# Block two's up products: a shared normalised operand for the last 16 of 22 weight slabs

## The chip, the core and the metric

The kernel runs on one core of one Trainium2 chip. The metric is the device time in microseconds (us) of one execution; lower is better. The core has five engines that run side by side and meet at semaphores: TensorE (PE, matrix products), VectorE (DVE), ScalarE (ACT), GpSimd (Pool) and SyncE (SP, which issues the weight DMAs here).

## What is computed

Two transformer blocks of two layers each, batch 1, 256 tokens, width 1024, all in 32-bit floats. The change touches only block two, whose layer applies the same gated feed-forward (a "macaron" half) before and after its mixer; so there are four such half-layers in the program:

```python
def rmsnorm(x, g):
    return x * rsqrt(mean(x * x, -1) + NORM_EPS) * g
def swiglu_2(x, w_gate, w_up, w_down):
    return (silu(x @ w_gate) * (x @ w_up)) @ w_down
for l in range(2):
    f = swiglu_2(rmsnorm(h, ln_ffn1[l]) * (1 + sc1) + sh1, ffn1_wg[l], ffn1_wu[l], ffn1_wd[l])
    h = h + 0.5 * gt1 * f
    ...  # mixer
    f = swiglu_2(rmsnorm(h, ln_ffn2[l]) * (1 + sc3) + sh3, ffn2_wg[l], ffn2_wu[l], ffn2_wd[l])
    h = h + 0.5 * gt3 * f
```

The inner width is 2816, that is 22 blocks of 128.

## The kernel before

Activations lie feature-major: 8 tiles of 128 features by 256 tokens (`k.hid`). A product in full precision is three products of split operands, written by `passes`: high by high, low by high, high by low. So every weight is split into a high and a low part. The weights come in slabs, in one fixed order over the whole program. For a slab, SP loads the raw weights, `act_hi` (L424) has ACT round them to the high part, `dve_lo` (L434) has DVE subtract to get the low part, and PE multiplies. There are 5 raw/low buffers and 3 high buffers.

Of each half-layer, 22 slabs are up slabs (128 gate columns and 128 up columns of the weights; 2 x 8 x 3 = 48 matmuls) and 16 are down slabs (33 matmuls each). PE fills two PSUM banks with an up slab, one with the gate half and one with the up half. There are two such pairs, and `pe_turn` lets PE begin slab t only once DVE has reported slab t-2 evacuated (`k.ev`).

The up products run before the norm is known. Their operand `k.x` (norm_in) is hidden times the modulation's scale, without the factor 1/rms of each token, and has two more columns that hold the shift. The products therefore have 258 columns, the last two of which are the shift's product with the weights. `dve_macaron` mends this for each slab i, from the 1/rms row `rstd`: two copies take the shift column (L1871), gate x rstd (L1872), up x rstd (L1873), after which `k.ev` is raised; ACT takes Silu with the shift as its bias (L1843); DVE adds the shift to the up half and multiplies by the gate (L1876); ACT copies to the high part (L1845) and then runs `act_hi` for a later slab; DVE subtracts for the low part (L1880), and begins the next turn with `dve_lo`, which waits for that `act_hi`.

Pool has only the sum of squares here (`pool_squares`, L1739), which it does while the down products run. Block one's second feed-forward (`dve_ffn_up`, `act_ffn_up`) has a normalised operand from the start; its products have 256 columns, ACT takes Silu straight from PSUM (L1155), and DVE multiplies Silu by the up half (L1174) and subtracts (L1178).

No scheduler is at work: each engine executes its instructions in the order in which these functions write them.

## Time and profile before

| what | us |
|---|---|
| median of 3 runs | 3343.29 |
| lowest, highest | 3340.78, 3350.56 |
| the profiled execution's own time | 3334.63 |
| its span, first to last instruction | 3333.3 |

The profile is of one execution, which is 8.7 us shorter than the median. Its mean granted TensorE clock is 0.943 of full speed. An engine's busy time says how long it had work; whether it sets the pace of a stretch is read from who waits for whom.

### The profile page before, as it was taken

The page shows a single profiled execution, that of the slowest core. Times are in us where ns is not written, and L with a number is a line of the kernel's source. Part 1 is how long each engine was busy: PE and PEld are TensorE (multiplying, and loading weights), DVE is VectorE, ACT ScalarE, POOL GpSimd, SP SyncE. Part 2 cuts the span into 40 slices and gives each one's busy share as a digit, 9 for nine tenths or more (in the row PEclk, how much of TensorE's full clock was granted, in tenths as well). Part 3 has the DMA queues.
Part 4 walks back from the last instruction along what each step waited for, and adds up shares of the span by engine and source line. Part 5 has one row for each costly group of instructions (what it writes and reads, how often), then busy time and mean ns, then how long its engine had stood idle before and what let it go on. Part 6 is the DMA issues. An engine that isn't in the chain of part 4 may idle for free.

```text
span 3333.3 us, 55236 instructions
## 1 busy us (share of the span) xinstructions
PE 3109.6 (93%) x23574; PEld 2900.9 (87%) x23574; DVE 2133.2 (64%) x3166; ACT 1198.8 (36%) x1533; POOL 275.8 (8%) x283
## 2 busy tenths in 40 slices
PE   7899999799999799899999989999999998999999
PEld 4777878699999777899899989889999998897998
DVE  5676776776677677555665854466656575545664
ACT  2112122344444233444444411444444442134543
POOL 5000000110102021101001020000000101000101
PEclk9889999799999899899999989999999998999999
DMA  7253443488999656466556612336575562222654
GB/s 271 89 178 106 154 142 94 147 247 242 253 249 281 220 165 207 133 178 190 150 159 165 171 32 71 99 117 177 157 198 156 162 173 68 65 84 82 181 161 126
DMA packets 746225, 524.77 MB, mean 157 GB/s; under 512 B 19242, under 2 KB 711660, under 8 KB 745852
## 3 DMA queue, kind: packets, MB, share of 16 engines
q1 hardware_dynamic: 741852, 516.18, 53.9%
q0 software_dynamic: 4128, 5.06, 0.5%
q8 instruction: 186, 3.05, 0.4%
q14 instruction: 59, 0.48, 0.0%
HBM read 520.07 MB, written 2.94 MB: 157 GB/s over the span
## 4 chain that ended last, share of the span: by engine, by line
PE 46%; issue 18%; DVE 10%; ACT 8%; DMA 1%; POOL 1%; SPq 0%; DVEq 0%; ACTq 0%; POOLq 0%
PE bank L454 11%; PE bank L456 11%; PE bank L455 11%; ACT weights_hi L424 6%; PE bank L1296 2%; DVE weights_lo L434 1%; ACT mac_gate L1843 1%; DVE mac_prod L1876 1%; DVE side_sums L541 1%; PE bank L2211 1%; PE bank L2223 1%; PE bank L2219 1%; PE bank L562 1%; DVE mac_gate L1872 1%; PE bank L1316 1%
## 5 line engine op out<-in xcount | busy, mean ns | idle before, releaser
L434 DVE TENSOR_TENSOR weights_lo<-weights_raw,weights_hi 128x2048 fp32r<-128x2048 f32 (+3 forms) x414 | 852.8, 2061 | 388.6 <-ACT weights_hi L424 388.4
L424 ACT ACTIVATE weights_hi<-weights_raw 128x2048 fp32r<-128x2048 f32 (+3 forms) x414 | 709.1, 1714 | 737.2 <-PE bank L456 663.1
L454 PE MATMUL bank<-norm_in_hi,weights_hi 128*128 128x258 f32 x1408 | 406.6, 289 | 16.1 <-DVE mac_prod L1873 10.4
L456 PE MATMUL bank<-norm_in_hi,weights_lo 128*128 128x258 f32 x1408 | 399.1, 283 | 0.0
L455 PE MATMUL bank<-norm_in_lo,weights_hi 128*128 128x258 f32 x1408 | 398.5, 283 | 0.0
L454 PE MATMUL bank<-ffn_in_hi,weights_hi 128*128 128x256 f32 x1184 | 348.0, 294 | 19.5 <-DVE ffn_in_lo L1088 8.6
L455 PE MATMUL bank<-ffn_in_lo,weights_hi 128*128 128x256 f32 x1184 | 344.0, 291 | 0.0
L456 PE MATMUL bank<-ffn_in_hi,weights_lo 128*128 128x256 f32 x1184 | 343.9, 290 | 0.0
L454 PE MATMUL bank<-mix_in_hi,weights_hi 128*128 128x256 f32 x960 | 286.2, 298 | 15.5 <-DVE conv_in L2090 6.4
L454 PEld LDWEIGHTS bank<-norm_in_hi,weights_hi 128*128 128x128 f32 x1408 | 267.5, 190 | 28.4 <-issue 27.3
L455 PE MATMUL bank<-mix_in_lo,weights_hi 128*128 128x256 f32 x960 | 278.7, 290 | 0.0
L456 PE MATMUL bank<-mix_in_hi,weights_lo 128*128 128x256 f32 x960 | 278.1, 290 | 0.0
L455 PEld LDWEIGHTS bank<-norm_in_lo,weights_hi 128*128 128x128 f32 x1408 | 269.6, 191 | 0.0
L456 PEld LDWEIGHTS bank<-norm_in_hi,weights_lo 128*128 128x128 f32 x1408 | 267.4, 190 | 0.0
L454 PEld LDWEIGHTS bank<-ffn_in_hi,weights_hi 128*128 128x128 f32 x1184 | 234.5, 198 | 22.7 <-issue 18.5
L541 DVE SCALAR_TENSOR_TENSOR side_sums<-side_weights,silu_c,side_sums 128x512 f32<-128x512 f32 (+2 forms) x261 | 241.0, 981 | 4.9 <-DMA side_weights<-in_ada_w 4.4
L455 PEld LDWEIGHTS bank<-ffn_in_lo,weights_hi 128*128 128x128 f32 x1184 | 234.8, 198 | 0.1
L456 PEld LDWEIGHTS bank<-ffn_in_hi,weights_lo 128*128 128x128 f32 x1184 | 234.3, 198 | 0.0
L454 PEld LDWEIGHTS bank<-mix_in_hi,weights_hi 128*128 128x128 f32 x960 | 190.2, 198 | 19.5 <-issue 12.5
L454 PE MATMUL bank<-mac_hi,weights_hi 128*128 128x256 f32 x704 | 198.5, 282 | 0.8 <-DVE weights_lo L434 0.8
L456 PE MATMUL bank<-mac_hi,weights_lo 128*128 128x256 f32 x704 | 198.6, 282 | 0.0
L455 PE MATMUL bank<-mac_lo,weights_hi 128*128 128x256 f32 x704 | 198.5, 282 | 0.0
(422 smaller groups left out, 6932.8 us busy)
## 6 DMA issues: line engine op xcount, KB each, us to landing
weights_raw<-in_ffn_w SPq DMA_DIRECT2D x132, 512.0 KB, 5.5
weights_raw<-in_w_in SPq DMA_DIRECT2D x120, 512.0 KB, 5.1
side_weights<-in_ada_w SPq DMA_DIRECT2D x86, 576.0 KB, 4.2
weights_raw<-in_ffn_wg SPq DMA_DIRECT2D x88, 512.0 KB, 4.0
weights_raw<-in_ffn_wu SPq DMA_DIRECT2D x88, 512.0 KB, 5.3
weights_raw<-in_ffn_wd SPq DMA_DIRECT2D x64, 704.0 KB, 4.6
weights_raw<-in_ffn_w SPq DMA_DIRECT2D x48, 704.0 KB, 6.1
weights_raw<-in_ret_w_in SPq DMA_DIRECT2D x24, 1024.0 KB, 6.1
```

Of the source, the lines that this page charges most:

```text
L424: k.s.activation(k.w_hi[s % HIGHS][:, 0:n], k.raw[s % RING][:, 0:n], ACT.Copy).then_inc(*k.hi.up())
L434: k.v.tensor_tensor(k.w_lo[s % RING][:, 0:n], k.raw[s % RING][:, 0:n], k.w_hi[s % HIGHS][:, 0:n].bitcast(F32), ALU.subtract).then_inc(*k.l ...
L454: k.te.matmul(out, l[0], r[0], start=first, stop=False)
L455: k.te.matmul(out, l[0], r[1], start=False, stop=False)
L456: return k.te.matmul(out, l[1], r[0], start=False, stop=last)
L541: k.v.scalar_tensor_tensor(acc, buf, col, acc, ALU.mult, ALU.add).then_inc(*raised.up())
L562: m = k.te.matmul(bank[:, v * n + c:v * n + c + 1], sums[:, v * width + c * P:v * width + (c + 1) * P], k.ones[:, 0:1], start=True, stop=True)
L1296: k.te.matmul(bank[:, 0:n], k.pair_q[r, tt * P:(tt + 1) * P], k.pair_k[r, 0:n], start=True, stop=False)
L1316: m = k.te.matmul(bank[r, 0:T], k.pair_v_all[:, s, self.at(e, n)], k.pair_pt[:, e, s, :], start=s == 0, stop=s == 3)
L1843: s.activation(g, g, ACT.Silu, bias=k.shifted[:, c:c + 1]).then_inc(*k.gated.up())
L1872: v.tensor_tensor(g, bank[0][:, 0:T], rstd, ALU.mult).then_inc(*k.gate_scaled.up())
L1876: v.scalar_tensor_tensor(x, x, k.shifted[:, (i % 2) * 2 + 1:(i % 2) * 2 + 2], g, ALU.add, ALU.mult).then_inc(*k.prod_ready.up())
```

## The change

For slabs 0 to 5 (`LATE = 6`) the products are as before. Behind them the normalised and modulated operand is made once, into new tiles mac_in_hi and mac_in_lo (`k.xn`), and slabs 6 to 21 use it, with 256 columns. Pool makes hidden x rstd for each of the 8 feature tiles (into `k.sq`, squares). ACT makes scale x that + shift twice, once rounded (mac_in_hi) and once in full (mac_in, `k.xv`, four buffers), two feature tiles at the end of each of its turns 0 to 3. The low part is a subtraction: of even tiles on Pool, of odd tiles on DVE at the end of its turns 1 to 4. For slabs 6 to 21 DVE and ACT then do what block one's second feed-forward does. The buffers that hold the operand are new; nothing else moves.

```diff
@@ -39,6 +39,7 @@
 NLEV = 7
 FILLS = 11
 BA_AT = 4
+LATE = 6
 LN_AT = {1: 8, 2: 3}
 TRI = 3 * P
 
@@ -341,6 +342,8 @@
         self.ln_added = self.sig("ln_added", "pool")
         self.ln_inverted = self.sig("ln_inverted", "dve")
         self.ln_spread = self.sig("ln_spread", "pe")
+        self.times_rms = self.sig("times_rms", "pool")
+        self.xn_lo = self.sig("xn_lo", "pool")
         self.slabs = weight_slabs(a)
         self.at_slot, self.side_at, self.side_prev = [], [], [None, None]
         self.sides = side_plan(a)
@@ -1820,7 +1823,11 @@
             pe_norm(k)
             continue
         for c in range(2):
-            m = feature_major(k, bank[c][:, 0:T + 2], w, c * P, x, slice(0, T + 2))
+            if i < LATE:
+                m = feature_major(k, bank[c][:, 0:T + 2], w, c * P, x, slice(0, T + 2))
+            else:
+                m = feature_major(k, bank[c][:, 0:T], w, c * P, k.xn, slice(0, T),
+                                  ready=(lambda n: (k.norm_lo if n % 2 else k.xn_lo).at(n // 2 + 1)) if i == LATE and c == 0 else None)
             if i == 1 and c == 0:
                 pe_spread(k)
         m.then_inc(*k.used.up())
@@ -1834,16 +1841,31 @@
         m.then_inc(*k.used.up())
 
 
-def act_macaron(k, following):
+def act_macaron(k, layer, j, following):
     s = k.s
+    sh = 3 * j * KD
     act_std(k)
     for i in range(KF):
         g, c = k.gate[i % 2][:, :], (i % 2) * 2
-        s.wait_ge(*k.gate_scaled.at(i + 1))
-        s.activation(g, g, ACT.Silu, bias=k.shifted[:, c:c + 1]).then_inc(*k.gated.up())
-        s.wait_ge(*k.prod_ready.at(i + 1))
+        if i < LATE:
+            s.wait_ge(*k.gate_scaled.at(i + 1))
+            s.activation(g, g, ACT.Silu, bias=k.shifted[:, c:c + 1]).then_inc(*k.gated.up())
+            s.wait_ge(*k.prod_ready.at(i + 1))
+        else:
+            s.wait_ge(*k.used.at(i + 1))
+            if i < LATE + 2:
+                s.wait_ge(*k.prod_ready.at(i - 1))
+            else:
+                s.wait_ge(k.ev.h, k.t0 + i - 1)
+            s.activation(g, k.GB[(k.t0 + i) % 2][0][:, 0:T], ACT.Silu).then_inc(*k.gated.up())
+            s.wait_ge(k.ev.h, k.t0 + i + 1)
         s.activation(k.mid[0][:, i, :], k.prod[i % 2][:, :], ACT.Copy).then_inc(*k.mid_hi.up())
         act_hi(k)
+        for n in (2 * i, 2 * i + 1) if 2 * i < KD else ():
+            sc, bi = (k.mods2[:, layer, at + n:at + n + 1] for at in (sh + KD, sh))
+            s.wait_ge(*k.times_rms.at(n + 1))
+            s.activation(k.xn[0][:, n, :], k.sq[:, n, :], ACT.Identity, scale=sc, bias=bi)
+            s.activation(k.xv[:, n % 4, :], k.sq[:, n, :], ACT.Identity, scale=sc, bias=bi).then_inc(*k.norm_hi.up())
     for i in range(4 * KD // 2):
         act_hi(k)
         if i % 4 == 1:
@@ -1861,12 +1883,19 @@
         dve_lo(k)
         if i == 0:
             dve_rms(k)
-            v.tensor_copy(rstd, k.AB[1][:, 0:T]).then_inc(*k.dve.up())
-            v.wait_ge(*k.dve.now())
+            v.tensor_copy(rstd, k.AB[1][:, 0:T]).then_inc(*k.affine.up())
+            v.wait_ge(*k.affine.at(1))
         turn = k.t0 + i
         bank, g, x = k.GB[turn % 2], k.gate[i % 2][:, :], k.prod[i % 2][:, :]
         v.wait_ge(*k.used.at(i + 1))
         v.wait_ge(*k.mid_lo.at(i - 1))
+        if i >= LATE:
+            v.wait_ge(*k.gated.at(i + 1))
+            v.tensor_tensor(x, g, bank[1][:, 0:T], ALU.mult).then_inc(*k.ev.up())
+            v.wait_ge(k.ev.h, turn + 1)
+            v.wait_ge(*k.mid_hi.at(i + 1))
+            v.tensor_tensor(k.mid[1][:, i, :], x, k.mid[0][:, i, :].bitcast(F32), ALU.subtract).then_inc(*k.mid_lo.up())
+            continue
         for c in range(2):
             v.tensor_copy(k.shifted[:, (i % 2) * 2 + c:(i % 2) * 2 + c + 1], bank[c][:, T:T + 1])
         v.tensor_tensor(g, bank[0][:, 0:T], rstd, ALU.mult).then_inc(*k.gate_scaled.up())
@@ -1878,6 +1907,11 @@
         v.wait_ge(*k.prod_ready.at(i + 1))
         v.wait_ge(*k.mid_hi.at(i + 1))
         v.tensor_tensor(k.mid[1][:, i, :], x, k.mid[0][:, i, :].bitcast(F32), ALU.subtract).then_inc(*k.mid_lo.up())
+        if 1 <= i <= KD // 2:
+            n = 2 * i - 1
+            v.wait_ge(*k.norm_hi.at(n + 1))
+            v.tensor_tensor(k.xn[1][:, n, :], k.xv[:, n % 4, :], k.xn[0][:, n, :].bitcast(F32), ALU.subtract).then_inc(
+                *k.norm_lo.up())
     for i in range(4 * KD // 2):
         dve_lo(k)
         if i % 2 == 1:
@@ -1893,6 +1927,16 @@
 
 
 def pool_macaron(k):
+    g, rstd = k.g, k.stat[0][:, 0:T]
+    g.wait_ge(*k.affine.at(1))
+    for n in range(KD + 2):
+        if n < KD:
+            g.tensor_tensor(out=k.sq[:, n, :], in0=k.hid[:, n, :], in1=rstd, op=ALU.mult).then_inc(*k.times_rms.up())
+        if n >= 2 and n % 2 == 0:
+            i = n - 2
+            g.wait_ge(*k.norm_hi.at(i + 1))
+            g.tensor_tensor(out=k.xn[1][:, i, :], in0=k.xv[:, i % 4, :], in1=k.xn[0][:, i, :].bitcast(F32),
+                            op=ALU.subtract).then_inc(*k.xn_lo.up())
     pool_squares(k, 1)
 
 
@@ -2635,9 +2679,11 @@
     m.at = inner
     k.mid = [m.take("mac_hi" + tag, [P, KF, T], F32R), m.take("mac_lo" + tag, [P, KF, T], F32R)]
     k.gate = [m.take(f"mac_gate{i}_{tag}", [P, T]) for i in range(2)]
+    k.xn = [m.take("mac_in_hi" + tag, [P, KD, T], F32R), m.take("mac_in_lo" + tag, [P, KD, T], F32R)]
+    k.xv = m.take("mac_in" + tag, [P, 4, T])
     k.prod = [m.take(f"mac_prod{i}_{tag}", [P, T]) for i in range(2)]
     sp_macaron(k)
-    act_macaron(k, following)
+    act_macaron(k, layer, j, following)
     dve_macaron(k, layer, j, following)
     pool_macaron(k)
     pe_macaron(k)
```


On DVE, a turn of a late slab before (names: weights_lo is `dve_lo`, ret_decay the shift columns, mac_gate, mac_prod and mac_lo the gate, the product and its low part; in brackets the semaphores it waits for):

```order
L434 TENSOR_TENSOR weights_lo_55<-weights_raw_50,weights_hi_59 128x2048 [waits weights_hi_ready]
L1871 COPY ret_decay<-bank 128x1 [waits mid_lo,weights_used]
L1871 COPY ret_decay<-bank 128x1
L1872 TENSOR_TENSOR mac_gate_00_15585<-bank,stat_69 128x256
L1873 TENSOR_TENSOR mac_prod_00_15587<-bank,stat_69 128x256
L1876 SCALAR_TENSOR_TENSOR mac_prod_00_15587<-mac_prod_00_15587,ret_decay,mac_gate_00_15585 128x256 [waits gated,banks_evacuated]
L1880 TENSOR_TENSOR mac_lo_15584<-mac_prod_00_15587,mac_hi_15583 128x256 [waits mid_hi,prod_ready]
```

and a late turn now:

```order
L437 TENSOR_TENSOR weights_lo_55<-weights_raw_50,weights_hi_59 128x2048 [waits weights_hi_ready]
L1894 TENSOR_TENSOR mac_prod_00_15590<-mac_gate_00_15585,bank 128x256 [waits gated,mid_lo,weights_used]
L1897 TENSOR_TENSOR mac_lo_15584<-mac_prod_00_15590,mac_hi_15583 128x256 [waits mid_hi,banks_evacuated]
L437 TENSOR_TENSOR weights_lo_56<-weights_raw_51,weights_hi_60 128x2048 [waits weights_hi_ready]
L1894 TENSOR_TENSOR mac_prod_00_15591<-mac_gate_00_15586,bank 128x256 [waits gated,mid_lo,weights_used]
L1897 TENSOR_TENSOR mac_lo_15584<-mac_prod_00_15591,mac_hi_15583 128x256 [waits mid_hi,banks_evacuated]
L437 TENSOR_TENSOR weights_lo_57<-weights_raw_52,weights_hi_61 128x2048 [waits weights_hi_ready]
```

Six instructions between two weights_lo became two. mac_prod now waits for Silu (gated) ahead of it, and `k.ev` is raised by it.

On ACT, the end of turn 0 and turn 1 of a half-layer before:

```order
L1843 ACTIVATE mac_gate_00_15586<-mac_gate_00_15586,ret_decay 128x256 [waits gate_scaled]
L1845 ACTIVATE mac_hi_15583<-mac_prod_00_15588 128x256 [waits prod_ready]
L424 ACTIVATE weights_hi_61<-weights_raw_51 128x2048 [waits weights_used,weights_arrived2]
L1843 ACTIVATE mac_gate_00_15585<-mac_gate_00_15585,ret_decay 128x256 [waits gate_scaled]
L1845 ACTIVATE mac_hi_15583<-mac_prod_00_15587 128x256 [waits prod_ready]
```

and the end of turn 1 with turn 2 now:

```order
L1862 ACTIVATE mac_hi_15583<-mac_prod_00_15591 128x256 [waits prod_ready]
L427 ACTIVATE weights_hi_61<-weights_raw_51 128x2048 [waits weights_used,weights_arrived2]
L1867 ACTIVATE mac_in_hi_15587<-squares,modulation_68 128x256 [waits times_rms]
L1868 ACTIVATE mac_in_15589<-squares,modulation_68 128x256
L1867 ACTIVATE mac_in_hi_15587<-squares,modulation_68 128x256 [waits times_rms]
L1868 ACTIVATE mac_in_15589<-squares,modulation_68 128x256
L1852 ACTIVATE mac_gate_00_15585<-mac_gate_00_15585,ret_decay 128x256 [waits gate_scaled]
L1862 ACTIVATE mac_hi_15583<-mac_prod_00_15590 128x256 [waits prod_ready]
L427 ACTIVATE weights_hi_59<-weights_raw_52 128x2048 [waits weights_used,weights_arrived3]
```

Four instructions now stand between weights_hi and the next turn's mac_gate.

On Pool, all that a half-layer adds, ahead of the sum of squares:

```order
L1934 TENSOR_TENSOR squares<-hidden_both,stat_69 128x256 [waits affine]
L1934 TENSOR_TENSOR squares<-hidden_both,stat_69 128x256 x2
L1938 TENSOR_TENSOR mac_in_lo_15588<-mac_in_15589,mac_in_hi_15587 128x256 [waits norm_hi]
L1934 TENSOR_TENSOR squares<-hidden_both,stat_69 128x256 x2
L1938 TENSOR_TENSOR mac_in_lo_15588<-mac_in_15589,mac_in_hi_15587 128x256 [waits norm_hi]
L1934 TENSOR_TENSOR squares<-hidden_both,stat_69 128x256 x2
L1938 TENSOR_TENSOR mac_in_lo_15588<-mac_in_15589,mac_in_hi_15587 128x256 [waits norm_hi]
L1934 TENSOR_TENSOR squares<-hidden_both,stat_69 128x256
L1938 TENSOR_TENSOR mac_in_lo_15588<-mac_in_15589,mac_in_hi_15587 128x256 [waits norm_hi]
```

Three products go first; from then on each subtraction waits for ACT's tile (norm_hi), with two products behind it. Before, none of these rows was there.

## Rows read from the trace of the kernel before

**Rows 1.** Tile norm_in_hi: two lines' instructions (ns); last, an idle time (us, times) and what ended it.

```profile
L454 PE MATMUL bank<-norm_in_hi,weights_hi x1408: 276/284/583, 1589.1 to 3256.2; 128*128 128x258 f32 x176
...
L1712 ACT ACTIVATE norm_in_hi<-hidden_both,modulation x32: 490/494/509, 1585.8 to 3124.9; 128x256 fp32r<-128x256 f32 x32
...
  DVE mac_prod L1873: 10.4, 64
```

**Rows 2.** Windows, slabs 6 to 21 of the four half-layers: stretch, length, busy time by engine.

```profile
core 0: us, PE busy (x) PEld busy (x) DVE busy (x) ACT busy (x) POOL busy (x), PEclk, DMA share, GB/s
1628.39:1726.91 98.52, 96.08 (x768) 93.42 (x769) 63.80 (x113) 43.44 (x50) 0.00 (x0) 1.00 0.58 158
...
sum 394.15, PE 384.39 PEld 373.78 DVE 255.16 ACT 173.83 POOL 0.00; mean PE 96.10 PEld 93.45 DVE 63.79 ACT 43.46 POOL 0.00
```

**Rows 3.** Windows: slabs 2 and 3 of the first half-layer; slabs 6-21 of block one.

```profile
1604.88:1616.42 11.54, 11.54 (x98) 11.54 (x97) 7.73 (x14) 4.95 (x5) 0.00 (x0) 1.00 0.67 183
1413.89:1505.03 91.14, 91.14 (x771) 91.14 (x769) 49.57 (x48) 41.18 (x48) 0.00 (x0) 1.00 0.63 174
```

**Rows 4.** Timeline of DVE, one turn: start, length, engine, line, instruction, idle before.

```profile
1606.63 2.29 DVE L434 TENSOR_TENSOR weights_lo<-weights_raw,weights_hi 128x2048 fp32r<-128x2048 f32 x1 [1.31 <-ACT weights_hi L424]
1608.84 0.21 DVE L1871 COPY ret_decay<-bank 128x1 f32<-128x1 f32 x2
1608.97 0.41 DVE L1872 TENSOR_TENSOR mac_gate<-bank,stat 128x256 f32<-128x256 f32 x1
1609.30 0.41 DVE L1873 TENSOR_TENSOR mac_prod<-bank,stat 128x256 f32<-128x256 f32 x1
1610.03 0.49 DVE L1876 SCALAR_TENSOR_TENSOR mac_prod<-mac_prod,ret_decay,mac_gate 128x256 f32<-128x256 f32 x1 [0.32 <-ACT mac_gate L1843]
1611.07 0.43 DVE L1880 TENSOR_TENSOR mac_lo<-mac_prod,mac_hi 128x256 fp32r<-128x256 f32 x1 [0.55 <-ACT mac_hi L1845]
1612.80 2.29 DVE L434 TENSOR_TENSOR weights_lo<-weights_raw,weights_hi 128x2048 fp32r<-128x2048 f32 x1 [1.31 <-ACT weights_hi L424]
```

**Rows 5.** Timeline of ACT, the same turn.

```profile
1609.42 0.51 ACT L1843 ACTIVATE mac_gate<-mac_gate,ret_decay 128x256 f32<-128x256 f32 x1 [2.83 <-DVE mac_gate L1872]
1610.55 0.42 ACT L1845 ACTIVATE mac_hi<-mac_prod 128x256 fp32r<-128x256 f32 x1 [0.62 <-DVE mac_prod L1876]
1610.87 1.90 ACT L424 ACTIVATE weights_hi<-weights_raw 128x2048 fp32r<-128x2048 f32 x1
```

**Rows 6.** Timeline of DVE in block one's second feed-forward.

```profile
1454.38 0.42 DVE L1174 TENSOR_TENSOR ffn_prod<-ffn_gate,bank 128x256 f32<-128x256 f32 x1 [0.69 <-ACT ffn_gate L1155]
...
1457.09 2.29 DVE L434 TENSOR_TENSOR weights_lo<-weights_raw,weights_hi 128x2048 fp32r<-128x2048 f32 x1 [1.30 <-ACT weights_hi L424]
```

**Rows 7.** Timeline of ACT there, the same turn.

```profile
1453.97 0.38 ACT L1155 ACTIVATE ffn_gate<-bank 128x256 f32<-128x256 f32 x1 [2.60 <-PE bank L456]
1454.84 0.42 ACT L1157 ACTIVATE ffn_hi<-ffn_prod 128x256 fp32r<-128x256 f32 x1 [0.49 <-DVE ffn_prod L1174]
1455.16 1.90 ACT L424 ACTIVATE weights_hi<-weights_raw 128x2048 fp32r<-128x2048 f32 x1
```

**Rows 8.** Timeline, down products of the first half-layer: one Pool addition beside VectorE.

```profile
1736.90 1.62 DVE L434 TENSOR_TENSOR weights_lo<-weights_raw,weights_hi 128x1408 fp32r<-128x1408 f32 x1
...
1737.57 1.54 POOL L1739 TENSOR_TENSOR square_sum<-square_sum,stat 128x256 f32<-128x256 f32 x1 [138.39 <-ACT stat L1714]
```

**Rows 9.** Lines 1725, 1739 and 434: duration min/median/max in ns.

```profile
L1725 DVE SCALAR_TENSOR_TENSOR norm_in_lo<-hidden_both,modulation,norm_in_hi x32: 473/479/964, 1588.5 to 3125.4; 128x256 fp32r<-128x256 f32 x32
...
L1739 POOL TENSOR_TENSOR square_sum<-square_sum,stat x56: 721/1467/2539, 1586.7 to 3320.9; 128x256 f32<-128x256 f32 x56
...
L434 DVE TENSOR_TENSOR weights_lo<-weights_raw,weights_hi x414: 285/2286/2831, 50.6 to 3309.6; 128x2048 fp32r<-128x2048 f32 x92, 128x1408 fp32r<-128x1408 f32 x37, 128x1024 fp32r<-128x1024 f32 x6, 128x1536 fp32r<-128x1536 f32 x3
```

**Rows 10.** Windows: 16 down slabs of the first half-layer, then of block one.

```profile
1726.91:1790.10 63.19, 62.98 (x530) 62.66 (x528) 33.70 (x31) 27.62 (x27) 13.42 (x7) 1.00 0.71 199
1510.73:1573.40 62.67, 62.67 (x531) 62.67 (x530) 33.31 (x30) 25.69 (x24) 10.17 (x10) 1.00 0.71 201
```

## Prediction

> **What bounds the kernel now.** I first asked which stretch the change can reach. It edits the up slabs 6 to 21 of four half-layers, and the windows give them: 98.52 us in the first, 394.15 in all four, 98.54 on the mean, at full granted clock [rows 2]. That is 12% of the span. TensorE executes there all the time by its busy column, so next I asked whether anything makes it wait. The tile view says yes: before 64 of the matmuls, the first of slabs 6 to 21 four times over, it sat until DVE's mac_prod (L1873), the instruction that frees a bank pair [rows 1]. The idle time shown, 10.4 us, understates it, because the modelled end of the matmul ahead covers part of each wait. A slab without the wait tells more: slabs 2 and 3 take 11.54 / 2 = 5.77 us [rows 3], while one turn from weights_lo to weights_lo takes 1612.80 - 1606.63 = 6.17 us [rows 4]. So PE loses 0.40 us a slab. It starts with a lead that the first five slabs use up; from slab 6 on it runs at the pace of the others.
>
> Which others? The timelines of DVE and ACT read together show one closed ring [rows 4, 5]: weights_lo to the shift copies 2.21, to mac_gate 0.13, to Silu's start on ACT 0.45, to the DVE multiply 0.61, to ACT's mac_hi 0.52, to weights_hi 0.32, to the next weights_lo 1.93. The sum is 6.17. Neither engine is full (DVE 63.80 of 98.52 us, ACT 43.44 [rows 2]); they wait for each other in turn.
>
> **What a late turn costs now.** Block one's second feed-forward executes the same instructions in the same order as the new late turns, with the same 48 matmuls of 256 columns. There Silu to DVE's product is 0.41, to ffn_hi 0.46, to weights_hi 0.32, to weights_lo 1.93 and through it 2.21 to 2.29 [rows 6, 7]. Two readings follow. The ring itself is 2.21 + 0.46 + 0.32 + 1.93 = 4.92 us, if Silu is done in time. From a slab's last matmul, the whole tail up to the end of weights_lo is 5.33 to 5.41 us. Both lie under what PE needs, so PE sets the pace, and the trace agrees: 16 slabs in 91.14 us, 5.70 each, with PE busy for all of it [rows 3]. The DMA is no obstacle to that pace: it moved 174 GB/s there, 158 in the stretch to be changed.
>
> Of the 0.47 to 0.48 us gained per slab, 0.40 is the wait and 0.075 the two columns (5.77 against 5.696, which is 1.6 ns a matmul). The Trainium skill ("TensorE: Matmul & The Clock Gate", Back-to-back issue gap) prices a column at 1/2.4 ns, so two would give 0.83 ns a matmul, and the columns of the whole change some 2 us less than I count; the measured slabs decide, and the sum goes by them.
>
> **Which slabs gain.** Slab 6 may start only when slab 4 is evacuated, and slab 7 only after slab 5, and both evacuations are old turns. Slab 6 thus still takes 6.17. The first new evacuation, that of slab 6, comes some 5.7 us after slab 7 began (from the end of mac_prod to the next weights_lo 3.09, then 2.21 and a product of 0.42 [rows 4, 6]), just when slab 8 can begin. So slabs 7 to 21 run at PE's pace: before, 98.54 - 6.17 = 92.37 us; after, 15 x 5.696 = 85.44. Gain 6.9 us per half-layer.
>
> **The start of the down products.** Because DVE is a slab behind, the old kernel's second and third down slabs wait for it. 16 down slabs took 63.19 us against 62.67 in block one, where DVE is not behind [rows 10]. Gain 0.5.
>
> **What is added, and where it lies.** ACT: four more activations in each of turns 0 to 3. The nearest row, the same kind on one tile with a scale, is 0.49 us [rows 1], so 2.0 us, behind weights_hi and ahead of the next Silu, where ACT sits idle for 2.83 [rows 5]: free, with 0.8 to spare, provided that Pool's products are there. DVE: one subtraction of 0.43 in turns 1 to 4, in the 1.31 that it idles before weights_lo [rows 4]: free. Its last one (tile 7) ends 1611.07 - 1609.30 + 2 x 0.43 - 0.41 = 2.2 us after slab 6 starts, and slab 6 asks for tile 7 after 21 of its matmuls, 2.5 us in (5.70 / 48 each): just in time, and if late, it is hidden by the 0.40 that slab 7 waits anyway.
>
> Pool: 8 products and 4 subtractions, 0.72 us each when undisturbed [rows 9]. Pool has nothing else there. Its price is what it does to DVE. Pool's addition at 1737.57 took 1.54 and ended 0.59 after the weights_lo beside it (1738.52) [rows 8]: it was held until that ended. The other way round, the DVE instruction with two SBUF inputs at L1725 takes 0.479 and up to 0.964 [rows 9], held by a Pool instruction in progress. In turns 1 to 3 Pool's subtraction is released while weights_lo executes, so it and two products (one in turn 3) start as weights_lo ends, a burst of some 2.2 us; the DVE multiply of the ring (L1876) starts 1.2 us after weights_lo ends, inside the burst. In turn 0 it meets the first three products. So four turns of five lose between 0 and 0.49 us; I take 0.40, as a burst back to back leaves hardly a gap: 1.6 us a half-layer. Such a loss delays the evacuation of slab 5, which slab 7 waits for, so it counts in full. The bounds: nothing if Pool always yields, and 4 x (0.49 + 0.55) = 4.2 if weights_lo is held as well each time (its maximum is 2831 ns over a median of 2286 [rows 9]).
>
> **Sum.** (6.9 + 0.5 - 1.6) x 4 = 23.2 us. The profiled execution of 3334.6 would become 3311.4; it lies 8.7 below the median of the three runs, and I apply the same saving to the median: 3343.3 - 23.2 = 3320.1. The bounds give 3343.3 - 29.6 = 3313.7 and 3343.3 - 12.8 = 3330.5.
>
> **Rivals.**
> - *Pool in DVE's way at full price.* Each early turn loses in both places: 4.2 a half-layer, 3330.5. For it speaks that weights_lo has been caught at 2831 ns; against it that Pool waits for ACT's tile when weights_lo begins, and is idle. The Trainium skill ("GPSIMD Engine Reference", Key points) says that Pool shares its SBUF interfaces with VectorE and contends with instructions that have two SBUF inputs, which would name both L1876 and weights_lo; the trace agrees that such instructions are held.
> - *Slower: the operand comes late.* ACT executes in order. If Pool's products reach it after weights_hi, its four activations hold the next Silu, and the ring grows by the lateness, in each of turns 1 to 3, and slab 6 waits as well. In turn 1 ACT asks for product 3 when weights_hi ends, 1612.77 [rows 5]; the burst starts at 1608.92 [rows 4] and product 3 is second in it, so it leaves at 1610.4, 2.4 us early. Each Pool instruction would have to take over 1.9 us instead of 0.72 for lateness to start, and the loss passes the gain of 7.4 a half-layer only when three turns and slab 6 lose 1.85 us each. The median of Pool's additions is 1.467 [rows 9], but beside long DVE instructions such as that of [rows 8], which the burst doesn't meet. With 3 us lost at each of the four places: 3343.3 + 4 x (12 - 7.4) = 3362.
> - *No change.* Another wait takes the place of the old one at the late slabs (a low part, a DMA) and holds the pace at about 6.1: 3340. Block one's 16 slabs without any wait speak against it.
> - *Pool always yields.* 3313.7.
>
> **How the numbers follow.** My forecast, the new pace with a small Pool loss (3314 to 3327), has 0.78; Pool at full price 0.12; no change 0.05; slower 0.05. For the range I take both bounds of the Pool cost, 3313.7 and 3330.5, and widen them by about 2 us, since the medians of three runs scatter (3340.78 to 3350.56): 3311 to 3333. That leaves out no change and slower. A measurement of this kernel tells 0.3% (10 us) from nothing; a saving of 12.8 still passes it. Faster 0.89, same 0.07, slower 0.04.
>
> **What the new profile would show.** Late slabs at 5.70 us, about 91.6 us for 16 of them in place of 98.5; the waits for mac_prod down from 64 to about 8 (slabs 6 and 7 of each half-layer); Silu's activation waiting for PE and not for DVE; L1876's early ones up to 0.96 us where Pool is active; Pool some 35 to 70 us busier, DVE busy less. The prediction is wrong if slabs 7 to 21 still wait, if ACT's Silu in turns 1 to 4 starts late behind the four activations, or if slab 6 waits for mac_in_lo by more than 0.4 us.

## The result, and the profile after

The changed kernel took 3307.34 us (median of 4 executions, 3298.29 to 3315.22), the kernel before 3346.93 beside it (4 executions, 3340.78 to 3350.98): a ratio of 0.9882, with a 95% interval of 0.9851 to 0.9914. It is 1.2% faster. That is the forecast direction, but more than the range allowed: 3307.3 lies 3.7 us below its lower end of 3311. The profiled execution took 3305.93, its span is 3304.6; before, it took 3334.63, so the two are 28.7 apart. Three executions of the kernels below took 4777 (both_orders), 7402 (late14) and 7754 us (both_again), for no known reason; they count in the medians of the table but not in its ratios, and the last is the one that both_again's profile fell on.

The page's head shows the engines' busy time and the shares of the chain that ended last:

```profile
span 3304.6 us, 55108 instructions
...
PE 3090.1 (94%) x23574; PEld 2892.9 (88%) x23574; DVE 2082.5 (63%) x2926; ACT 1220.6 (37%) x1597; POOL 330.6 (10%) x331
...
PE 55%; issue 14%; DVE 9%; ACT 4%; DMA 2%; POOL 1%; SPq 0%; DVEq 0%; ACTq 0%; POOLq 0%
```

Pool is 54.8 us busier than the 275.8 of before (48 instructions more), DVE 50.7 less than its 2133.2, PE 19.5 less than its 3109.6. Pool and DVE stand in the prediction's list of what the profile would show. So do early multiplies of DVE (L1876, now L1905) of up to 0.96 us, and these didn't come: the longest took 0.58. In the chain PE rose to 55% from 46%.

The windows of slabs 6 to 21 answer to [rows 2]. Shown are the first half-layer and the sum of all four:

```profile
core 0: us, PE busy (x) PEld busy (x) DVE busy (x) ACT busy (x) POOL busy (x), PEclk, DMA share, GB/s
1634.53:1726.29 91.76, 91.54 (x769) 91.35 (x770) 52.77 (x56) 42.65 (x51) 0.00 (x0) 1.00 0.61 170
...
sum 367.02, PE 366.00 PEld 365.28 DVE 211.01 ACT 170.55 POOL 0.00; mean PE 91.50 PEld 91.32 DVE 52.75 ACT 42.64 POOL 0.00
```

16 slabs take 91.75 us where they took 98.54; the prediction said about 91.6. DVE's busy time fell from 63.80 to 52.77. The down products of the first half-layer answer to [rows 10]:

```profile
1726.29:1789.10 62.81, 62.81 (x530) 62.60 (x528) 31.15 (x25) 25.99 (x25) 13.69 (x7) 1.00 0.72 202
```

They take 62.81 instead of 63.19: 0.4 gained, where the prediction said 0.5. The tile view of the new operand answers to [rows 1]:

```profile
L457 PE MATMUL bank<-mac_in_hi,weights_hi x1024: 274/281/360, 1634.5 to 3228.1; 128*128 128x256 f32 x171
...
  DVE mac_prod L1902: 1.0, 4
...
  ACT mac_gate L1860: 110.0, 48
```

The waits for DVE's product fell from 64 to 4 (the prediction said about 8). Those four are the starts of slab 7. At slab 6 the view shows no wait, since the modelled end of the matmul ahead covers it; but slab 6 starts 0.40 after that matmul, where matmuls otherwise start 0.12 apart. Silu (L1860) now waits for PE, 48 times of 64, and no longer for DVE. So the engines have changed roles, as expected: PE sets the pace, and ACT and DVE wait for it. PE's own timeline, cut into slabs, gives from slab 4 on of the first half-layer 5.88, 6.13, 6.22, 5.76, 5.72, and then 5.70 each (before: 5.79 for slab 4, and about 6.18 from slab 5 on). A slab's length includes the wait ahead of the next, so that 6.22 holds slab 7's.

How DVE comes from the old pace to the new one shows in its timeline in the middle of the stretch:

```profile
1668.27 2.29 DVE L437 TENSOR_TENSOR weights_lo<-weights_raw,weights_hi 128x2048 fp32r<-128x2048 f32 x1 [1.31 <-ACT weights_hi L427]
1670.48 0.41 DVE L1894 TENSOR_TENSOR mac_prod<-mac_gate,bank 128x256 f32<-128x256 f32 x1
...
1673.18 2.29 DVE L437 TENSOR_TENSOR weights_lo<-weights_raw,weights_hi 128x2048 fp32r<-128x2048 f32 x1 [1.31 <-ACT weights_hi L427]
1675.73 0.42 DVE L1894 TENSOR_TENSOR mac_prod<-mac_gate,bank 128x256 f32<-128x256 f32 x1 [0.26 <-ACT mac_gate L1860]
```

From weights_lo to weights_lo it takes 1673.18 - 1668.27 = 4.91 us, the new ring of 4.92. It still catches up there, 0.79 a slab. One turn later the product waits for Silu, and Silu for PE: from about slab 12 on DVE is no longer behind.

**Where all of the gain is.** The four half-layers, each from its first up matmul to the end of its down products, took 201.11, 197.77, 198.38 and 197.74 us before, 795.0 together, and take 193.92, 190.57, 190.54 and 190.57 now, 765.6. That is 29.4 us less. 0.65 of it isn't the change's: the third one's down products were slower before (3.96 us a slab in place of 3.92). The medians differ by 39.6, so the question is what the rest of the program did. Windows of the three stretches outside, of before:

```profile
0.00:1589.08 1589.08, 1452.79 (x9511) 1303.63 (x9511) 1081.01 (x1386) 521.57 (x670) 163.70 (x190) 0.93 0.63 186
1790.19:2254.90 464.71, 430.52 (x3836) 408.73 (x3837) 280.45 (x506) 162.03 (x235) 26.28 (x25) 0.94 0.36 101
2650.89:3122.10 471.21, 436.18 (x3836) 414.13 (x3837) 280.27 (x506) 161.97 (x235) 26.39 (x25) 0.92 0.36 100
sum 2525.00, PE 2319.49 PEld 2126.49 DVE 1641.73 ACT 845.58 POOL 216.37; mean PE 773.16 PEld 708.83 DVE 547.24 ACT 281.86 POOL 72.12
```

And of after:

```profile
0.00:1595.18 1595.18, 1458.46 (x9511) 1309.66 (x9511) 1080.88 (x1386) 521.77 (x670) 162.96 (x190) 0.92 0.63 186
1789.10:2251.92 462.82, 428.40 (x3837) 407.19 (x3838) 280.47 (x506) 161.94 (x235) 26.28 (x25) 0.94 0.37 102
2632.86:3100.68 467.82, 433.02 (x3837) 411.12 (x3837) 280.04 (x506) 162.05 (x235) 26.36 (x25) 0.93 0.36 101
sum 2525.82, PE 2319.88 PEld 2127.97 DVE 1641.38 ACT 845.76 POOL 215.60; mean PE 773.29 PEld 709.32 DVE 547.13 ACT 281.92 POOL 71.87
```

Single stretches move by 6 us up and 3 down, the sum by 0.8. Outside the half-layers nothing was gained. The ten us between 29.4 and 39.6 are what these few executions happened to take; the two profiled ones differ by 28.7.

### The profile page after: what moved, and what is told of

Same layout as the page of the kernel before. It is cut to its first block, busy times and chain, and to the rows that moved or that the text cites. A ratio compares the mean times of both kernels' runs of the same rounds, so it can differ in the third digit from the quotient of the medians.

```text
span 3304.6 us, 55108 instructions
## 1 busy us (share of the span) xinstructions
PE 3090.1 (94%) x23574; PEld 2892.9 (88%) x23574; DVE 2082.5 (63%) x2926; ACT 1220.6 (37%) x1597; POOL 330.6 (10%) x331
## 4 chain that ended last, share of the span: by engine, by line
PE 55%; issue 14%; DVE 9%; ACT 4%; DMA 2%; POOL 1%; SPq 0%; DVEq 0%; ACTq 0%; POOLq 0%
PE bank L457 14%; PE bank L458 14%; PE bank L459 14%; ACT weights_hi L427 3%; PE bank L1299 2%; DVE weights_lo L437 1%; DVE side_sums L544 1%; PE bank L2255 1%; PE bank L2267 1%; PE bank L2263 1%; PE bank L565 1%; DVE side_sums_odd L544 1%; PE bank L1304 1%; DMA weights_raw<-in_ffn_w 1%; PE bank L1302 1%
## 5 line engine op out<-in xcount | busy, mean ns | idle before, releaser
L457 PE MATMUL bank<-mac_in_hi,weights_hi 128*128 128x256 f32 x1024 | 289.0, 282 | 1.5 <-DVE mac_prod L1902 1.0
L459 PE MATMUL bank<-mac_in_hi,weights_lo 128*128 128x256 f32 x1024 | 288.4, 282 | 0.0
L458 PE MATMUL bank<-mac_in_lo,weights_hi 128*128 128x256 f32 x1024 | 288.4, 282 | 0.0
L457 PEld LDWEIGHTS bank<-ffn_in_hi,weights_hi 128*128 128x128 f32 x1184 | 234.5, 198 | 23.2 <-issue 19.0
L457 PEld LDWEIGHTS bank<-mac_in_hi,weights_hi 128*128 128x128 f32 x1024 | 192.8, 188 | 2.9 <-issue 2.9
L459 PEld LDWEIGHTS bank<-mac_in_hi,weights_lo 128*128 128x128 f32 x1024 | 192.8, 188 | 0.0
L458 PEld LDWEIGHTS bank<-mac_in_lo,weights_hi 128*128 128x128 f32 x1024 | 192.8, 188 | 0.0
```

Source lines behind the costliest of these rows:

```text
L457: k.te.matmul(out, l[0], r[0], start=first, stop=False)
L458: k.te.matmul(out, l[0], r[1], start=False, stop=False)
L459: return k.te.matmul(out, l[1], r[0], start=False, stop=last)
```

## The experiments

Each ran beside the kernel before on the same chip. The stated half-layer is from the profile, and is one that the slower pace of PE (also at the end) doesn't touch; before it is 197.74 us long, after the change 190.56.

| kernel | median us (executions) | ratio to before, 95% | half-layer us |
|---|---|---|---|
| after_again | 3310.79 (6) | 0.9911, 0.9889 to 0.9933 | 190.54 |
| before_again | 3336.04 (12) | 0.9989, 0.9974 to 1.0005 | 197.73 |
| added_alone | 3340.47 (12) | 0.9995, 0.9984 to 1.0005 | 197.80 |
| order_alone | 3310.54 (5) | 0.9900, 0.9883 to 0.9917 | 190.71 |
| order_again | 3310.70 (5) | 0.9900, 0.9879 to 0.9922 | 190.71 |
| both_orders | 3309.36 (6) | 0.9898, 0.9874 to 0.9921 | 189.46 |
| both_again | 3310.85 (6) | 0.9886, 0.9861 to 0.9911 | none |
| late14 | 3336.05 (10) | 0.9980, 0.9962 to 0.9998 | 194.42 |
| late_wide | 3318.38 (5) | 0.9940, 0.9919 to 0.9962 | 191.71 |
| pool_shifted | 3317.29 (4) | 0.9929, 0.9905 to 0.9953 | 191.28 |
| pool_twice | 3310.57 (1) | one execution | 190.56 |
| pool_mid | 3313.12 (1) | one execution | 191.81 |

### How large is the gain: the two kernels once more

after_again is the changed kernel, before_again the one before, unchanged.

> The changed kernel once more, with more rounds. Theory 1: all of the gain lies in the four half-layers, which are 7.2, 7.2, 7.8 and 7.2 us shorter in the two profiles, 29.4 together; the ratio should come out near 1 - 29.4/3345 = 0.9912, and the rest of the 39.6 us between the medians is scatter. Theory 2: stretches outside the half-layers, the mixers above all, gain too: then about 38 to 40 us, ratio 0.9882, again.

> The kernel of before against itself: how far two medians of one kernel differ. Ratio 1.000; if the interval is wider than 0.003, the 10 us between the two theories of the size can't be told from it. The profile should repeat the four half-layers within 0.3 us, and differ by several us in the stretches between them, where the granted clock falls.

The half-layers came back as 193.93, 190.54, 190.55, 190.56 and as 201.11, 197.76, 197.73, 197.73: they repeat within 0.05 us. The one exception is the third of before, 198.38 and now 197.73: its down slabs ran at the slower pace the first time. The ratio 0.9911 stands for 29.7 us of 3342.4, the 29.4 of the half-layers. Another 10 us from elsewhere (0.9882) lie just outside its interval, and the windows above, where the rest of the program gained nothing, speak against them more strongly. The kernel before against itself gave 0.9989, with an interval of 0.0031: by the limit that its expectation sets, such a timing can hardly tell 10 us.

### The operand made, but not used

```diff
-LATE = 6
+LATE = 22
```

> LATE = 22: the operand is made (Pool, ACT, DVE) but no slab uses it, so every turn is an old one. Theory A (Pool costs next to nothing here): DVE's product at L1905 is held in turn 0 by 0.09 us and not in turns 1 to 3; a half-layer is longer by 0.1 us, the kernel by 0.4 us: ratio 1.000. Rival (as predicted, 0.40 in each of four turns): 6.4 us slower, ratio 1.002. What it says on the whole: the added work alone gives nothing.

Nothing is gained, and nothing is lost: slabs 6 to 21 take 98.52, and a half-layer 0.06 more than before. The view of the line that Pool can hold, L1905 (before: L1876), in this kernel:

```profile
L1905 DVE SCALAR_TENSOR_TENSOR mac_prod<-mac_prod,ret_decay,mac_gate x88: 483/485/578, 1606.5 to 3259.8; 128x256 f32<-128x256 f32 x88
```

Of 88 instructions the longest takes 0.578, 0.09 over the median, and it occurs in turn 0 of a half-layer alone. So the 12 instructions on Pool, 16 on ACT and 4 on DVE cost next to nothing, not the 1.6 us that I had put on Pool.

### The order of the instructions alone, without a new operand

The kernel before, with ACT's mac_hi behind the next weights_hi, and DVE's mac_lo behind the next weights_lo. So the DVE multiply and mac_hi no longer stand between Silu and weights_hi:

```diff
         s.activation(g, g, ACT.Silu, bias=k.shifted[:, c:c + 1]).then_inc(*k.gated.up())
+        act_hi(k)
         s.wait_ge(*k.prod_ready.at(i + 1))
         s.activation(k.mid[0][:, i, :], k.prod[i % 2][:, :], ACT.Copy).then_inc(*k.mid_hi.up())
-        act_hi(k)
...
-        dve_lo(k)
         if i == 0:
+            dve_lo(k)
             dve_rms(k)
...
+        if i < KF - 1:
+            dve_lo(k)
```

> The kernel of before with one reordering and no new operand: ACT rounds the next weights right behind Silu, ahead of mac_hi, and DVE makes their low part right behind L1876, ahead of mac_lo. If the ring of waits between DVE and ACT is the cause, it shrinks to Silu to weights_hi 0.45, to weights_lo 1.93, 2.21 through it, mac_lo 0.35, copies 0.13 and 0.13, to Silu 0.45: 5.65 us, below the 5.77 of a slab with 258 columns. Then PE sets the pace in all 22 slabs: 0.40 x 16 + 0.35 + 0.46 for the down products = 7.2 us a half-layer, 29 us, ratio 0.9914, without any of the change. Rival: what helps is that DVE and ACT have less to do or that the products are narrower; then a late slab stays at 6.18 and the time the same.

The window of slabs 6 to 21, and DVE's timeline while it still catches up:

```profile
1641.20:1733.58 92.38, 92.38 (x771) 92.38 (x770) 64.11 (x114) 40.83 (x48) 0.00 (x0) 1.00 0.61 169
```

```profile
1651.65 2.29 DVE L434 TENSOR_TENSOR weights_lo<-weights_raw,weights_hi 128x2048 fp32r<-128x2048 f32 x1 [1.25 <-ACT weights_hi L424]
...
1657.12 2.29 DVE L434 TENSOR_TENSOR weights_lo<-weights_raw,weights_hi 128x2048 fp32r<-128x2048 f32 x1 [1.25 <-ACT weights_hi L424]
```

And ACT's:

```profile
1654.78 0.51 ACT L1843 ACTIVATE mac_gate<-mac_gate,ret_decay 128x256 f32<-128x256 f32 x1 [2.85 <-DVE mac_gate L1872]
1655.19 1.90 ACT L424 ACTIVATE weights_hi<-weights_raw 128x2048 fp32r<-128x2048 f32 x1
```

The new ring is read off the starts: weights_lo and mac_lo up to the copies 1654.20 - 1651.65 = 2.55 (the copies start at 1654.20), copies and mac_gate to Silu 0.58, Silu 0.41, weights_hi 1657.12 - 1655.19 = 1.93. The sum is 5.47, and below PE's 5.77, at which all slabs from 2 on are. (I expected 5.65; 0.13 of that was a second step for the copies, which lies inside the other steps.) The half-layer gains 7.03 of the change's 7.18, and DVE does as much work as before (64.11 busy against 63.80 in [rows 2]). So what cost the 0.40 a slab was the length of the closed ring, which the order sets, and not how much DVE has to do. The new operand isn't needed for that.

### Both: the change with the early turns in that order

```diff
+            act_hi(k)
             s.wait_ge(*k.prod_ready.at(i + 1))
...
-        act_hi(k)
+        if i >= LATE:
+            act_hi(k)
...
-        dve_lo(k)
+        if i == 0 or i > LATE:
+            dve_lo(k)
...
+        dve_lo(k)
+        v.wait_ge(*k.prod_ready.at(i + 1))
+        v.wait_ge(*k.mid_hi.at(i + 1))
+        v.tensor_tensor(k.mid[1][:, i, :], x, k.mid[0][:, i, :].bitcast(F32), ALU.subtract).then_inc(*k.mid_lo.up())
```

> The changed kernel, with its six early turns reordered: weights_hi right behind Silu, weights_lo ahead of mac_lo, the extra subtraction ahead of weights_lo. Theory: slabs 4, 5 and 6 took 5.88, 6.13 and 6.22 us in the changed kernel because DVE is late there; now 5.77, 5.77 and 5.70: 1.0 us a half-layer, 4 us in all against the changed kernel, ratio to before about 0.990. Rival: the extra work in turns 1 to 4 (ACT 2.3 us, DVE 0.4, Pool in DVE's way) lengthens the reordered ring beyond 5.77; then slabs 4 to 6 stay near 6.1 and nothing is gained.

In the profile no slab from 2 on is held up: slabs 2 to 5 take 5.77, 6 to 21 take 5.70, and a half-layer 189.46, 1.1 less than the change and 1.25 less than the order alone. Slabs 6 to 21, with PE busy throughout:

```profile
1622.42:1713.55 91.13, 91.13 (x770) 91.13 (x769) 52.73 (x56) 42.41 (x50) 0.00 (x0) 1.00 0.62 171
```

Over four that is 761.2 against 766.2, 5 us. The executions can't tell it: the intervals of the two ratios overlap almost wholly. Both were run again with their own expectations:

> The new operand with reordered early turns once more, on the same chip as the reordering alone. By the half-layers of the profiles (192.8, 189.5, 189.5 and 189.5 us) it is 33 us faster than before, ratio 0.9901, and 5 us faster than the reordering alone: 1.3 us a half-layer from the narrower products.

> The reordering alone once more: by its half-layers (194.1, 190.7, 190.7 and 190.7 us) 28 us faster than before, ratio 0.9916. If the two can't be told apart in time, the intervals overlap and only the profiles separate them.

0.9886 and 0.9900, with intervals of 0.004 to 0.005 across: still not told apart. By the profile both_orders is the best kernel of the study; by the timing that stays open.

### Where in the stretch the gain comes from: only the last 8 slabs

```diff
-LATE = 6
+LATE = 14
```

> LATE = 14: eight of the sixteen late slabs are old ones again. Theory (gain per slab): slabs 6 to 13 go back to 6.18 and slab 14 is held as slab 6 is now, so 8 x 0.48 = 3.85 us a half-layer come back, 15.4 in all; the half-layers are 13.9 us shorter than before in place of 29.4. Rival (the gain lies in the end of the up products or outside them): the gain stays near the full one.

Windows of slabs 6 to 13 and 14 to 21 of the second half-layer:

```profile
2305.91:2355.30 49.39, 48.15 (x385) 46.73 (x385) 32.33 (x57) 21.82 (x25) 0.00 (x0) 1.00 0.63 171
2355.30:2401.50 46.20, 45.91 (x385) 45.73 (x385) 27.31 (x31) 21.78 (x27) 0.00 (x0) 1.00 0.56 155
```

The old slabs keep 6.17, the new ones take 5.77 on the mean, with their own slow first one (PE busy 45.91 of 46.20). This half-layer gained 3.35 of 7.20: the 3.85 of the eight slabs that stayed old came back as expected. The other three ran at PE's slower pace from the late slabs on (198.94, 195.56 and 195.51 us), so the profile has 10.6 us gained in all, not the 13.9 expected. The timing (0.9980, 6.7 us, with 12.7 us as the most that its interval allows) falls short of the 13.9 too. That is in part the slower pace; how much of it every execution had, the one profile doesn't show.

### What the two columns are worth

258 columns in the late slabs; the two extra are copied from the old operand, and their results are read by nobody.

```diff
-                m = feature_major(k, bank[c][:, 0:T], w, c * P, k.xn, slice(0, T),
+                m = feature_major(k, bank[c][:, 0:T + 2], w, c * P, k.xn, slice(0, T + 2),
...
+        if i == 0:
+            s.activation(k.xn[0][:, :, T:T + 2], k.x[0][:, :, T:T + 2].bitcast(F32), ACT.Copy)
...
+        if i == 1:
+            v.tensor_copy(k.xn[1][:, :, T:T + 2], k.x[1][:, :, T:T + 2].bitcast(F32))
```

> The changed kernel with 258 columns in the late slabs too (two idle columns, their content copied and never read); DVE and ACT have their new turns. Theory: a late slab takes 5.77 in place of 5.70, without waits: 16 x 0.075 = 1.2 us a half-layer, 4.8 in all. By the price of 1/2.4 ns a column it would be 16 x 48 x 0.83 ns = 0.64 a half-layer, 2.6 in all. If the columns were the main thing, the time would go back by over 20 us.

The window of its slabs 6 to 21 in the second half-layer:

```profile
2293.36:2386.27 92.91, 92.70 (x768) 92.53 (x769) 52.76 (x56) 42.70 (x51) 0.00 (x0) 1.00 0.61 168
```

92.91 against 91.75: 1.16 us for 768 matmuls, 1.5 ns each. Over the four half-layers the columns are 4.6 us of the 29.4, and the wait is the rest. The Trainium skill ("TensorE: Matmul & The Clock Gate", Back-to-back issue gap) gives 1/2.4 ns a column for an isolated matmul at full clock; an estimate from it is 0.83 ns for two columns, or 0.64 us for these 768 matmuls. The trace, where a weight load goes with each matmul, shows nearly twice that.

### Pool's price, by moving its burst

In the change Pool's subtraction is held by weights_lo, and its products follow. The timelines of Pool and of DVE in turns 0 and 1 of the first half-layer:

```profile
1608.78 2.34 POOL L1934 TENSOR_TENSOR squares<-hidden_both,stat 128x256 f32<-128x256 f32 x3 [5.64 <-DVE stat L1886]
1613.83 1.86 POOL L1938 TENSOR_TENSOR mac_in_lo<-mac_in,mac_in_hi 128x256 fp32r<-128x256 f32 x1 [2.71 <-ACT mac_in L1868]
1615.66 1.64 POOL L1934 TENSOR_TENSOR squares<-hidden_both,stat 128x256 f32<-128x256 f32 x2
```

```profile
1609.94 0.58 DVE L1905 SCALAR_TENSOR_TENSOR mac_prod<-mac_prod,ret_decay,mac_gate 128x256 f32<-128x256 f32 x1 [0.32 <-ACT mac_gate L1852]
...
1612.81 2.29 DVE L437 TENSOR_TENSOR weights_lo<-weights_raw,weights_hi 128x2048 fp32r<-128x2048 f32 x1 [1.31 <-ACT weights_hi L427]
...
1616.21 0.48 DVE L1905 SCALAR_TENSOR_TENSOR mac_prod<-mac_prod,ret_decay,mac_gate 128x256 f32<-128x256 f32 x1 [0.32 <-ACT mac_gate L1852]
...
1617.60 0.42 DVE L1913 TENSOR_TENSOR mac_in_lo<-mac_in,mac_in_hi 128x256 fp32r<-128x256 f32 x1
```

The subtraction takes 1.86, since it sits until weights_lo ends. The first product then starts at 1615.66, and L1905 at 1616.21, 0.55 later: it takes its plain 0.48. In turn 0 it starts 0.45 after the second of the three products, and takes 0.58. So what may count is the phase, by which I mean how long after the start of Pool's instruction DVE's starts. To test it, a memset on Pool (0.31 us) behind each subtraction delays the two products. (The edit, and those of the next two kernels, are against the changed kernel.)

```diff
+            g.wait_ge(*k.pool.now())
+            g.memset(k.square_sum[:, :], 0.0).then_inc(*k.pool.up())
+    g.wait_ge(*k.pool.now())
```

> The changed kernel with one Pool memset (0.31 us) behind each of Pool's subtractions, so that the two products that follow start later. Theory A: a Pool instruction holds DVE's instruction with two SBUF inputs only during its first 0.55 us; L1905 starts 0.55 after a Pool product in turns 1 to 3 by the accident of its place, 0.22 after it now, and should be held by 0.32 (0.80 us in place of 0.48) in those three turns: slab 7 starts 1.0 us later, 3.9 us in all. Theory B: Pool does not hold this instruction at all: L1905 stays at 0.48 in turns 1 to 3, and the time the same.

Pool's and DVE's timelines of pool_shifted in turn 2, and the line's minimum, median and maximum:

```profile
1620.74 0.31 POOL L1941 MEMSET square_sum<- 128x256 f32 x1
1621.01 1.64 POOL L1934 TENSOR_TENSOR squares<-hidden_both,stat 128x256 f32<-128x256 f32 x2
```

```profile
1621.31 0.73 DVE L1905 SCALAR_TENSOR_TENSOR mac_prod<-mac_prod,ret_decay,mac_gate 128x256 f32<-128x256 f32 x1 [0.31 <-ACT mac_gate L1852]
```

```profile
L1905 DVE SCALAR_TENSOR_TENSOR mac_prod<-mac_prod,ret_decay,mac_gate x24: 484/646/730, 1608.6 to 3150.1; 128x256 f32<-128x256 f32 x24
```

Now L1905 starts 1621.31 - 1621.01 = 0.30 after the product, and takes 0.73: held for 0.24. The half-layer is 0.72 longer, which is three turns of 0.24. I expected 0.22 and a hold of 0.32; the memset moved the products by 0.25 and not by 0.31, and 0.30 + 0.24 is 0.54, as 0.22 + 0.32 would have been.

With two memsets (`for _ in range(2)` ahead of the same two lines):

> Two memsets behind each of Pool's subtractions. One memset moved the two products by 0.25 us and L1905 was held by 0.24. Theory A (held until 0.54 us after the start of the Pool instruction, and only if it starts inside that time): the products start another 0.27 later, L1905 some 0.03 us after one of them, and is held by about 0.5 us (0.98 in place of 0.48) in turns 1 to 3: 1.5 us a half-layer, with turn 0 1.6, which is the 0.40 a turn that the prediction charged. If the product starts just after L1905, Pool waits instead and L1905 stays at 0.48. Theory B (the hold is a fixed 0.24 whenever they overlap): 0.72 again.

Line L1905 of pool_twice, and the timelines of DVE and Pool in turn 2:

```profile
L1905 DVE SCALAR_TENSOR_TENSOR mac_prod<-mac_prod,ret_decay,mac_gate x24: 483/486/574, 1604.4 to 3147.7; 128x256 f32<-128x256 f32 x24
```

```profile
1623.06 0.49 DVE L1905 SCALAR_TENSOR_TENSOR mac_prod<-mac_prod,ret_decay,mac_gate 128x256 f32<-128x256 f32 x1 [0.32 <-ACT mac_gate L1852]
```

```profile
1622.49 0.67 POOL L1942 MEMSET square_sum<- 128x256 f32 x2
1623.12 1.02 POOL L1934 TENSOR_TENSOR squares<-hidden_both,stat 128x256 f32<-128x256 f32 x1
```

L1905 is at its plain 0.486, and Pool waits: its product starts at 1623.12, just behind L1905 (1623.06), and takes 1.02 instead of 0.74. The half-layer is 190.56, the change's own. So in these runs whichever of the two started first went first.

With one memset of 256 columns and one of 32, the phase falls in between:

> Behind each of Pool's subtractions a memset of 256 columns and one of 32, so that the two products start later than with one full memset and earlier than with two. L1905 should then start 0.05 to 0.2 us after a Pool product starts. Theory A (held until 0.54 us after the start of the Pool instruction): L1905 takes 0.8 to 0.97 us in turns 1 to 3, a half-layer is 1.1 to 1.5 us longer than in the changed kernel. If the product still starts after L1905, it stays at 0.48.

```profile
L1905 DVE SCALAR_TENSOR_TENSOR mac_prod<-mac_prod,ret_decay,mac_gate x24: 485/736/914, 1610.9 to 3148.7; 128x256 f32<-128x256 f32 x24
```

```profile
1623.69 1.64 POOL L1934 TENSOR_TENSOR squares<-hidden_both,stat 128x256 f32<-128x256 f32 x2
```

```profile
1623.81 0.91 DVE L1905 SCALAR_TENSOR_TENSOR mac_prod<-mac_prod,ret_decay,mac_gate 128x256 f32<-128x256 f32 x1 [0.32 <-ACT mac_gate L1852]
```

By the records' starts the product begins 0.12 ahead of L1905, which takes 0.89 to 0.91 in turns 1 to 3, held for about 0.42; slabs 4 and 5 of the undisturbed half-layer take 6.60 and 6.55, and it is 1.25 longer than the change's. So a price near my 1.6 does exist, but at another phase than the change has.

## Why the prediction was right on the mechanism and wrong on the number

- **The bound**: right, though PE is busy for 96.08 of the 98.52 us by its busy column, and not all the time as I wrote. The ring of DVE and ACT held PE by 0.40 a slab. order_alone, which shortens that ring and nothing else, brings 5.77 us slabs.
- **The new ring of 4.92, and PE's pace of 5.70**: right; 4.91 was seen, and 91.75 for 16 slabs against some 91.6.
- **Which slabs gain**: right. Slab 6 takes 6.22 with slab 7's wait in it, and from slab 8 on PE is free. late14 gave back 3.85 us for eight slabs in its one half-layer at PE's full pace, as expected.
- **Start of the down products**: right, 0.4 to 0.5 where I said 0.5.
- **The two columns**: 1.5 ns a matmul against the 1.6 I counted.
- **ACT's four activations**: they start 0.49 apart, 2.0 us in all, though each takes 0.58 in the record, and 0.86 of idle time stays ahead of Silu where I said 0.8:

```profile
1612.68 0.58 ACT L1867 ACTIVATE mac_in_hi<-squares,modulation 128x256 fp32r<-128x256 f32 x1
1613.17 0.59 ACT L1868 ACTIVATE mac_in<-squares,modulation 128x256 f32<-128x256 f32 x1
...
1614.15 0.59 ACT L1868 ACTIVATE mac_in<-squares,modulation 128x256 f32<-128x256 f32 x1
1615.60 0.51 ACT L1852 ACTIVATE mac_gate<-mac_gate,ret_decay 128x256 f32<-128x256 f32 x1 [0.86 <-DVE mac_gate L1901]
```

- **Pool's price in DVE's way, 1.6 us a half-layer**: this is the step that failed, a term of the sum that was mis-sized. I wrote "I take 0.40, as a burst back to back leaves hardly a gap". It measured 0.1, in turn 0 alone. I had asked only whether the two overlap. What decides is when DVE's instruction starts inside Pool's: the hold fell from about 0.42 us at 0.12 us after Pool's start to 0.24 at 0.30, 0.09 at 0.45 and nothing at 0.55. The products start 0.56 after weights_lo ends, and L1905 1.11 after it, so they meet at 0.55 in each of turns 1 to 3. The 6.0 us of this term are nearly all of the 6.2 between the forecast gain of 23.2 and the 29.4 of the half-layers. The rival "Pool always yields", 3313.7, gives its number, though not its reason: Pool doesn't always yield (pool_mid).
- **What rows of before already said of it**: the Pool addition of [rows 8] ended 0.59 after weights_lo, and by [rows 4] L1876 starts 1610.03 - 1608.92 = 1.11 after it (I wrote 1.2), so the phase to expect was 0.52. And the trace of before shows what a phase does. Pool starts here at 2257.86, and a DVE instruction of usually 0.479 at 2258.21:

```profile
2257.86 1.62 POOL L1739 TENSOR_TENSOR square_sum<-square_sum,stat 128x256 f32<-128x256 f32 x2 [2.69 <-ACT stat L1714]
```

```profile
2258.21 0.66 DVE L1725 SCALAR_TENSOR_TENSOR norm_in_lo<-hidden_both,modulation,norm_in_hi 128x256 fp32r<-128x256 f32 x1 [0.23 <-ACT norm_in_hi L1712]
```

  At 0.36 after Pool's start (0.357 before rounding) it was held by 0.18, which is 0.54 together. I had used only the line's longest, 0.964.
- **The range**: Pool's term alone doesn't explain why the measured median is outside it, because the lower bound, 3313.7, already had Pool at nothing. With the measured gain the sum is 3343.3 - 29.4 = 3313.9, inside the range, and yet the median was 3307.3, some 6 us lower. For the profiled execution the same sum gives 3334.6 - 29.4 = 3305.2, and it took 3305.9. So what put the median outside was the scatter of medians, for which I had widened the range by only 2 us. The same changed kernel gave 3307.3 and 3310.8, the same kernel before 3336.0 to 3346.9 in different sets; two sets on one chip, 12 and 23 executions, were 6.4 apart. This second error is one of size too.
- Nothing of "the operand comes late" or "no change" was seen: slab 6 waited for no tile of the operand.

The gain has two parts: the columns (4.6 us) and the wait in the ring, with the down start that follows from it (the other 24.8, which also holds the 0.65 named above). Only the columns need the operand made by Pool, ACT and DVE. It also removes the wait, through the shorter turns that it allows, but moving two calls does that too.

## What to carry to other kernels

When two engines wait for each other in turn, write down the closed ring with its starts, and ask first which instruction could leave it by a change of order: here two moved calls gave 28.8 of 29.4 us. Price contention between Pool and VectorE by the phase of their starts, not by whether they overlap, and take the phase from the event that releases both (here the end of weights_lo). Where the medians of the same kernel wander by 5 to 10 us, read small gains from the profile's stretches, which repeat within 0.05 us, and give the range of a timed median that width.

## What the runs showed of the hardware

- **Pool's product held L1905 only in the product's first 0.54 us.** Pool's products (two SBUF inputs, 128x256) take 0.74. L1905, a DVE instruction with two SBUF inputs, was held for about 0.54 - t when it started t after one (0.42, 0.24 and 0.09 us at 0.12, 0.30 and 0.45), and not at all at 0.55. In the trace of before the same sum, of L1725 or weights_lo beside a Pool instruction, is 0.54 to 0.61 where Pool's takes 0.73 to 0.79, and 0.68 to 0.78 where Pool's own is held up and takes 0.88 or 0.92. Pool's memset, which reads nothing, did not hold it: 0.486 at 0.20 after one (pool_twice). The Trainium skill ("GPSIMD Engine Reference", Key points) says that VectorE's instructions with two SBUF inputs contend with GpSimd, and the trace agrees; that section gives no size. DVE's instructions that read PSUM (L1901, L1902) took 0.41 to 0.42 in each of these kernels, beside Pool's subtraction too. The other way round Pool's subtraction was held until weights_lo ended, and finished 0.59 after it, as in [rows 8].
- **PE showed a 1% slower pace at full granted clock.** In some half-layers, different ones in different profiles, late slabs take 5.76 instead of 5.70 and down slabs 3.96 instead of 3.92. Where the ring sets the pace of the up slabs, it shows in the down slabs alone (the third half-layer of before). Down products of pool_mid's first and second half-layer, both at a clock of 1.00:

```profile
1729.49:1793.02 63.53, 63.53 (x530) 63.31 (x528) 31.20 (x25) 26.01 (x25) 13.78 (x7) 1.00 0.71 199
2383.84:2446.66 62.82, 62.82 (x532) 62.82 (x531) 33.60 (x32) 28.94 (x33) 10.80 (x7) 1.00 0.69 198
```

  The cause is open.
- **Block one and the mixers scatter.** Block one took 1583.5 to 1602.3 us in the profiles. In order_alone's (1602.3) PE was busy 1467.4 us at a mean granted clock of 0.92, in both_orders' (1583.5) 1448.6 at 0.93. So the longer one goes with more time at the lower granted clock, and the totals agree: of the changed kernel's executions the shortest (3298.29) had a mean granted clock of 0.946, the longest (3315.22) 0.940.
